# Scatter-add into the residual's table, and the last norm's roots on GpSimd, in a one-core decoder step with 32 experts

## What is computed

```
h2 = rms_norm(x, norm2_g) * (1 + sc2) + sh2
...
return (jax.nn.silu(xb @ w1[e]) * (xb @ w3[e])) @ w2[e]
...
contrib = y_rows[dest] * w_sorted[:, None]
return jnp.zeros((t, d), y_rows.dtype).at[tok_sorted].add(contrib)
...
x = x + g2 * y.reshape(n, t, d)
...
y_prompt = rms_norm(xp, final_norm_g)
y_sample = rms_norm(xs, final_norm_g)
```

## Time and profile before

| | |
|---|---|
| median of 3 runs | 1634.91 us (1634.49 to 1636.73) |
| the profiled execution | 1632.61 us |
| its span, first to last instruction | 1630.9 us |
| PE busy in the span | 1577.2 us (97%) |
| DVE, ACT, POOL busy | 1264.6, 804.3, 300.4 us |
| bytes moved | 368.71 MB, mean 226 GB/s |
| granted PE clock, mean | 0.993 |

### The profile page before, as it was taken

One profiled execution on the slowest core, in us unless ns is written; L12 is line 12 of the kernel. 1 busy time (PEld: TensorE's weight loads), 2 busy tenths in 40 slices (PEclk: granted clock), 3 DMA queues, 4 the chain that ended last, 5 costly groups with the idle time before them and its releaser, 6 DMA issues.

```text
span 1630.9 us, 23361 instructions
## 1 busy us (share of the span) xinstructions
PE 1577.2 (97%) x9163; PEld 1347.6 (83%) x9163; DVE 1264.6 (78%) x1683; ACT 804.3 (49%) x867; POOL 300.4 (18%) x267
## 2 busy tenths in 40 slices
PE   6999999999999999999999999999999999999993
PEld 3777788788889999999899977888888888888871
DVE  4668887755838898877455469999999999999956
ACT  4222232334333223223243357778878888878832
POOL 2310000000000000002000205655432232233210
PEclk9999999999999999999999999999999999999997
DMA  9965222424434222224223648999999999999938
GB/s 339 317 205 169 86 82 87 149 78 148 127 97 162 92 84 79 79 85 144 59 78 97 232 176 320 379 405 400 392 388 383 383 377 384 378 381 394 363 149 319
DMA packets 217073, 368.71 MB, mean 226 GB/s; under 512 B 16338, under 2 KB 164898, under 8 KB 191610
## 3 DMA queue, kind: packets, MB, share of 16 engines
q1 hardware_dynamic: 198972, 332.41, 56.9%
q0 software_dynamic: 17344, 32.64, 5.6%
q10 hardware_dynamic: 646, 2.15, 0.3%
HBM read 353.63 MB, written 31.31 MB: 236 GB/s over the span
## 4 chain that ended last, share of the span: by engine, by line
PE 89%; DVE 6%; DMA 2%; DVEq 1%; issue 1%; ACT 1%; SPq 0%; POOLq 0%
PE z L2712 16%; PE z L2714 16%; PE z L2713 16%; PE z L825 7%; PE z L823 7%; PE z L824 7%; PE z L840 4%; PE z L842 4%; PE z L841 4%; PE q L814 2%; PE q L2603 2%; PE q L2622 1%; DVE conv L2134 1%; DMA ada_h<-in_w_ada_dram 1%; PE q L831 1%
## 5 line engine op out<-in xcount | busy, mean ns | idle before, releaser
L1146 DVE TENSOR_TENSOR wl<-wr,whr 128x2048 fp32r<-128x2048 f32 x198 | 446.5, 2283 | 0.0
L2712 PE MATMUL z<-h_hi,w_hi 128*128 128x272 f32 (+1 forms) x1248 | 407.2, 326 | 2.3 <-DVE h_lo L1953 1.8
L2714 PE MATMUL z<-h_hi,w_lo 128*128 128x272 f32 (+1 forms) x1248 | 402.9, 323 | 0.0
L2713 PE MATMUL z<-h_lo,w_hi 128*128 128x272 f32 (+1 forms) x1248 | 401.9, 322 | 0.0
L992 ACT ACTIVATE whr<-wr 128x2048 fp32r<-128x2048 f32 x198 | 374.9, 1911 | 51.9 <-PE z L825 51.3
L1953 DVE TENSOR_TENSOR w_lo<-w_raw,w_hi 128x1024 fp32r<-128x1024 f32 (+1 forms) x168 | 179.5, 1069 | 138.3 <-ACT w_hi L1652 138.3
L2712 PEld LDWEIGHTS z<-h_hi,w_hi 128*128 128x128 f32 x1248 | 234.9, 188 | 28.2 <-issue 7.3
L2714 PEld LDWEIGHTS z<-h_hi,w_lo 128*128 128x128 f32 x1248 | 234.7, 188 | 16.5
L2713 PEld LDWEIGHTS z<-h_lo,w_hi 128*128 128x128 f32 x1248 | 235.1, 188 | 15.7 <-issue 0.2
L823 PE MATMUL z<-whr,xTh 128*128 128x512 f32 x528 | 209.1, 396 | 0.1
L825 PE MATMUL z<-wl,xTh 128*128 128x512 f32 x528 | 206.4, 391 | 0.0
(11 more groups left out here) (452 smaller groups left out, 2278.7 us busy)
## 6 DMA issues: line engine op xcount, KB each, us to landing
wr<-in_w_dram SPq DMA_DIRECT2D x198, 1024.0 KB, 8.8
w_raw<-in_w_in_dram SPq DMA_DIRECT2D x104, 512.0 KB, 3.7
ada<-in_w_ada_dram SPq DMA_DIRECT2D x6, 2048.0 KB, 14.9
w_raw<-in_w_branch_dram SPq DMA_DIRECT2D x48, 256.0 KB, 2.7
w_raw<-in_w_out_dram SPq DMA_DIRECT2D x16, 512.0 KB, 3.9
yin<-y_rows SPq DMA_DIRECT2D x16, 512.0 KB, 9.8
ada_h<-in_w_ada_dram SPq DMA_DIRECT2D x2, 2048.0 KB, 14.8
ada_u<-in_w_ada_dram SPq DMA_DIRECT2D x2, 2048.0 KB, 9.8
```

The costliest lines, as they stand in the source:

```text
L1146: return dve.tensor_tensor(out, a, b, op)
L2712: pe.matmul(out, w_hi[w][:, k, :], hi[:, k, t0:t1], start=(k == 0), stop=False)
L2713: pe.matmul(out, w_hi[w][:, k, :], lo[:, k, t0:t1], start=False, stop=False)
L2714: last = pe.matmul(out, w_lo[w][:, k, :], hi[:, k, t0:t1], start=False, stop=(k == kn - 1))
```

## The change

Four edits are made together.

1. A block's results are added to the residual's own table `x1_dram` by the transfer itself (`compute_op=ALU.add`), at the row's index in the token list instead of the two-place list. As two experts can name one row, each scatter first waits until the one before has landed. `y_dram` is gone. The sample rows of the table are first zeroed by a POOL transfer, and the samples' residual goes to a small table `x1s_dram`, since their gate is applied at the end. At the end SP loads one tile of finished sums for each row tile, 9 transfers for 18, and the load of `x1a` falls away, and so do PE's sums and DVE's `row_sum`, except for the samples' product and sum.
2. The inverse roots are made by POOL in three batches of three tiles, 15 instructions each, with the tiles in the order 0, 1, 8, 2 to 7. ACT squares every tile straight from `yin`.
3. `factor_columns` and `factors_read` stand one pair of products later.
4. `bias_rows` stands before `gated(NB_B, GB0, 4)` instead of behind it.

```diff
             def scatter_dma(s, col, done):
-                pool.indirect_dma_start(y_dram, bass.IndirectOffsetOnAxis(ap=col, axis=0), ysb[s][:], None,
-                                        bounds_check=2 * TPAD - 1, oob_is_err=False).then_inc(done, 16)
+                pool.indirect_dma_start(x1_dram, bass.IndirectOffsetOnAxis(ap=col, axis=0), ysb[s][:], None,
+                                        bounds_check=TOK - 1, oob_is_err=False, compute_op=ALU.add).then_inc(done, 16)
...
             def scatter(b):
                 pool.wait_ge(m_y, b + 1)
-                scatter_dma(b % 2, tb0[:, b:b + 1] if b < NE else xcol[:, 0:1], m_sc[b % 2])
+                if b:
+                    pool.wait_ge(m_sc[(b - 1) % 2], 16 * ((b + 1) // 2))
+                scatter_dma(b % 2, tok0[:, b:b + 1] if b < NE else xtok[:, 0:1], m_sc[b % 2])
...
             for t in F_ORDER:
-                for k in range(2):
-                    r0 = t * P + k * TPAD
-                    sp.dma_start(yin[0:f_rows[t], t, k, :], y_dram[r0:r0 + f_rows[t], :]).then_inc(rows_in[t], 16)
+                sp.dma_start(yin[0:f_rows[t], t, :], x1_dram[t * P:t * P + f_rows[t], :]).then_inc(rows_in[t], 16)
...
-            sp.wait_ge(m_c, 8 + RN * (NCH // RN - 1) + 1)
-            sp.dma_start(x1a[:], x1_dram[0:SEQ, :].rearrange("(t p) d -> p t d", p=P)).then_inc(f_par, 16)
...
+            pool.dma_start(x1_dram[SEQ:TOK, :].rearrange("r (a c) -> r a c", c=64),
+                           blk64[0:SMP, 64:P].unsqueeze(1).to_broadcast([SMP, D // 64, 64])).then_inc(x1_out, 16)
...
+            def roots(n0, n):
+                v, y, t = fv[:, n0:n], fy[:, n0:n], ft[:, n0:n]
+                pool.wait_ge(f_sq, n)
+                pool.tensor_scalar(v, fss[:, n0:n], 1.0 / D, EPS, ALU.mult, ALU.add)
+                pool.drain()
+                pool.tensor_scalar(y.bitcast(I32), v.bitcast(I32), -0.5, float(MAGIC), ALU.mult, ALU.add)
+                pool.drain()
+                pool.tensor_scalar(v, v, -0.5, None, ALU.mult)
+                for _ in range(3):
+                    pool.drain()
+                    pool.tensor_tensor(t, y, y, ALU.mult)
...
+                last.then_inc(f_r, 1)
...
                     elif g and i == 2 * PT - 2:
                         spatial(PT, SMP)
+                    elif g:
                         factor_columns()
...
-                gated(NB_B, GB0, 4)
                 if g:
                     bias_rows()
+                gated(NB_B, GB0, 4)
                 inverse()
```

More of the change, by code:

```diff
@@ L112, in sb @@
             return t
-        F_PE, F_ORDER = (1, 3, 5, 7), (8, 1, 0, 3, 2, 5, 4, 7, 6)
-        F_BATCH = (F_ORDER[0:4], F_ORDER[4:9])
+        F_ORDER = (8, 0, 1, 2, 3, 4, 5, 6, 7)
+        F_BATCH = ((0, 1, 8), (2, 3, 4), (5, 6, 7))
+        F_ROWS = sum(F_BATCH, ())
         TG = [HALF, HALF + SMP]
@@ L309, in build @@
         top[0] = o
-        yin, o = at("yin", [P, NT, 2, D], F32, low_end)
+        yin, o = at("yin", [P, NT, D], F32, low_end)
         assert o <= whi_at
@@ L582, in build @@
         o_i, o_w, o_c, o_x, o_sc = (sem(n) for n in ("o_i", "o_w", "o_c", "o_x", "o_sc"))
-        f_par, g2_in, f_mm, m_w, f_sum, f_sq, f_y, f_out = (
-            sem(n) for n in ("f_par", "g2_in", "f_mm", "m_w", "f_sum", "f_sq", "f_y", "f_out"))
+        f_par, g2_in, m_w, f_sum, f_sq, f_r, f_y, f_out = (
+            sem(n) for n in ("f_par", "g2_in", "m_w", "f_sum", "f_sq", "f_r", "f_y", "f_out"))
         W_IN = ((v_out, 16), (mc_in, 32))
@@ L661, in moe_sync @@
                 r0 = (PT + t) * P
-                sp.dma_start(x1_dram[r0:r0 + rows, :], xres[0:rows, t, :]).then_inc(last_out[t % 2], 16)
+                dst = x1_dram[r0:r0 + rows, :] if t < PT else x1s_dram
+                sp.dma_start(dst, xres[0:rows, t, :]).then_inc(last_out[t % 2], 16)
             sp.wait_ge(r_ok, 1)
@@ L805, in moe_gpsimd @@
                     pool.wait_ge(m_y, n_)
-                    scatter_dma(0, xcol[:, 0:1], o_sc)
+                    pool.wait_ge(m_sc[0], 16 * ((NB + 1) // 2))
+                    pool.wait_ge(m_sc[1], 16 * (NB // 2))
+                    scatter_dma(0, xtok[:, 0:1], o_sc)
+            def roots(n0, n):
[9 more added lines that the diff above has]
+                    pool.tensor_tensor(t, y, y, ALU.mult)
+                    pool.drain()
+                    pool.tensor_tensor(t, v, t, ALU.mult)
+                    pool.drain()
+                    pool.tensor_scalar(t, t, 1.5, None, ALU.add)
+                    pool.drain()
+                    last = pool.tensor_tensor(y, t, y, ALU.mult)
+                last.then_inc(f_r, 1)
+            n = 0
+            for batch in F_BATCH:
+                roots(n, n + len(batch))
+                n += len(batch)
             pool.wait_ge(st_out, 16 * (3 + 2 * NS))
@@ L956, in moe_tensor @@
                         step_down(pe, c, whr[4 + c], wl[XS[4 + c]])
[L957 to L970, removed]
         def moe_scalar(act):
@@ L1060, in moe_scalar @@
                     factors(0)
[L1062 to L1076, removed]
+            for n, t in enumerate(F_ROWS):
+                rows = f_rows[t]
+                if t == NT - 1:
+                    act.wait_ge(f_sum, 1)
+                else:
+                    results_in(act, t)
+                if n >= 2:
+                    act.wait_ge(f_sq, n - 1)
+                act.activation(xg[n % 2][0:rows, :], yin[0:rows, t, :], ACT.Square,
+                               accum_out=fss[0:rows, n:n + 1]).then_inc(f_sq, 1)
         def pick_groups(dve, t0, t1):
@@ L1332, in moe_vector, with row_out @@
                     result(0)
[L1334 to L1339, removed]
-                results_in(dve, t)
[L1341 to L1372, removed]
+            dve.wait_ge(f_par, 16 * (2 + NS))
+            results_in(dve, NT - 1)
+            acc = yin[0:SMP, NT - 1, :]
+            tt(acc, acc, g2s[:], ALU.mult)
+            dve.drain()
+            tt(acc, acc, x1s[0:SMP, :], ALU.add).then_inc(f_sum, 1)
+            def row_out(t):
+                rows, out, n = f_rows[t], yin[0:f_rows[t], t, :], F_ROWS.index(t)
+                results_in(dve, t)
+                dve.scalar_tensor_tensor(out, out, fy[0:rows, n:n + 1], fgb[0:rows, :], ALU.mult, ALU.mult).then_inc(f_y, 1)
+            for n, batch in enumerate(F_BATCH):
+                dve.wait_ge(f_r, n + 1)
+                for t in batch:
+                    row_out(t)
         w_in_v = w_in[0].rearrange("(k p) c -> p k c", p=P)
@@ L1819, in _ @@
                 if g:
-                    act.wait_ge(x1_out, 16 * PT)
+                    act.wait_ge(x1_out, 16 * (PT + 1))
                 for i in range(CW):
@@ L2354, in _ @@
                 if g:
[L2355 removed]
+                    dve.wait_ge(x1_out, 16 * (PT + 1))
                 for i in range(CW):
@@ L2430, in _ @@
                         spatial(PT, SMP)
+                    elif g and i == 2 * PT - 1:
                         factors_read()
```

14 lines of the change are left out of this document (6 added, 8 removed).

## The result

The changed kernel takes **1644.71 us** (median of 5 runs, 1643.4 to 1646.24), the kernel before 1636.19 beside it on the same chip: a ratio of 1.0052 (95% interval 1.004 to 1.0064). It is 8.5 us slower, where 1620 was forecast. The profiled execution took 1646.14 us, its span is 1644.3: 13.4 more than before.

What follows compares the result with a forecast made beforehand. PE was taken as the bound, queues close behind, with one chain after the last scatter. The terms -2.2 - 3.1 + 1.0 - 11.0 = -15.3 gave 1619.6 us against the median 1634.9, rounded to 1620; range 1612 to 1637.

Steps and rivals of the forecast that it cites:

- Edits 3 and 4: Dense part: two waits of PE for late DVE reads go away, -2.2 and -3.1 us.
- The scatters beside PE: Expert part: the queues' reserve absorbs the adding scatters, cost 0; 0 to 5 us if partitions decide the engine.
- the map: Expert part: partitions 0 to 63 belong to engines 0 to 7, so 1.26 us a block instead of 0.63.
- price "as a gather": Expert part: adding reads destination rows as a gather does, +0.63 us of each engine a block.
- The reserve of "9 to 15 us": Expert part: backlog the chunk loads can bear before PE waits, 9 to 15 us, of which 1.5 used.
- the expert part becomes bound by its transfers: Rival, expert part: transfers make PE wait, whole gain lost at 1.73 us more a block, 1657 at 2.5; chance 0.13.
- Its formula: Expert part: at x us more per block, waiting is 29x - 3.6 - 19.3 less the reserve, 12.
- The new wait on POOL's queue: Expert part: each scatter waits for the one before, which lands with 8 us to spare; cost 0.
- The last scatter: Start of the end chain: reading before writing adds a DRAM trip, +1.0 us, between 0 and 3.98.
- The end: Behind the last scatter's landing: 32.2 us against 43.2, -11.0, with POOL's batches taking 4.7, 5.5 and 5.5 us.
- GpSimd's roots: Rival, at the end: POOL's instructions are 0.5 us apart, the end 6.9 us longer, 1626.5; chance 0.14.

Runs made afterwards that it cites:

- e1: The kernel before with only the two mended PE waits in the dense part (edits 3 and 4): 1628.13 us, ratio 0.9959.
- e2: The kernel after with scatters that write and do not add: 1630.4 us, ratio 0.9972.
- e6: The kernel before with a block's rows dealt over 16 groups of four partitions, as a control: 1634.92 us, ratio 0.9997.
- e4: The kernel after with a memset and one GpSimd integer instruction on scratch columns right behind the last scatter's issue: 1637.08 us, ratio 1.001.
- e10: e4 with float views in place of integer views in the new GpSimd instruction: 1636.72 us, ratio 1.0006.
- e11: The kernel after with e4's two instructions placed ahead of the loop over blocks, none behind the last scatter: 1643.95 us, ratio 1.0053.
- e7: e4 with DVE starting its multiplications only when all three batches of roots are made: 1640.5 us, ratio 1.0024.
- e3: The kernel after with a block's rows dealt over 16 groups of four partitions: 1630.52 us, ratio 0.9973.

## Why the prediction was wrong

Against the profiled execution it said 1617.3; 1646.14 came: 28.8 us too low. Step by step:

- *Edits 3 and 4* (-5.3): right. All blocks up to the ninth are 5.2 us early, and alone the mends gave 7.1 in the medians, 4.4 to 8.8 by its interval (e1; 4.6 in its trace, at every block).
- *The scatters beside PE* (0, with 0 to 5 us for the rows in the low partitions): this is the first step that failed, by 14.5 us. I had the mechanism only as a possibility, and undersized each of its terms.

  The addition costs 1.38 us a block and not 0.63 (e2). Two things that the trace of before held are missing in the 0.63. It was read from 1300 to 1500 us, where a block moves 57 rows; from 1018 to 1130 us it moves about 80, and queue 0 has 10.0% (the same in e6), so the same working gives 0.100 x 17.75 / 2 = 0.89. And it is the mean of 16 engines: if the low partitions belong to eight of them, as the map has it, these carry 64 of 80 rows, 1.6 times as much, which as an estimate is 1.42, close to the 1.38. The price "as a gather" was sound, for adding raised queue 0's share by 0.94 and 0.59 us a block in the two stretches, against 0.89 and 0.63 by that price; the stretch and the mean were not.

  The reserve of "9 to 15 us" is its low end: the landing stops at 24 to 26, 8 to 9.5 above the 16.5 at the start. In the later blocks I let the queues catch up by 0.92 us a block, as the earlier trace rows showed it; in e2 it is (12.6 - 7.7) / 6 = 0.82 (7.7 is the median of the chunks issued from 1231 us). With 1.38 that leaves 0.56 a block, and with the smaller later blocks less, but the blocks are 18.44 - 17.75 = 0.69 behind the plan. Why was not tried, and stays open.

  Of the rivals, "the expert part becomes bound by its transfers", at 0.13, has the mechanism. Its formula had the same faulty terms: at x = 1.38 it gives 29 x 1.38 - 3.6 - 19.3 - 12 = 5.1 us, and 14.5 were lost. By itself that loss would have ended near 1619.6 + 14.5 = 1634, at the time of before; slower than before it became only with the end.
- *The new wait on POOL's queue* (0): right, e2 has it and loses nothing.
- *The last scatter* (+1.0 between 0 and 3.98): +2.1 in the trace; against a plain one at the same place (3.2, e2) adding costs 2.9.
- *The end* (-11.0, that is 32.2 us behind the last landing): the second step that failed, by 13.0 us; it took 45.2. The loads and squares came as said, the first batch began 9.5 us behind the landing (9.4 forecast). But the first batch took 12.7 us for 4.7: its instructions were 0.35 us apart, near the 0.31 taken, and the gap of 7.7 was not counted (e4, e10 and e11 place it). The earlier trace rows took the spacing from two places without a gap, though the same POOL showed 6.74 and 5.02 us between them and 8.31 at 965 us. The other two took 8.0 for 5.5: I had a factor for POOL beside DVE, 1.2, from long work at another place, and missed that each of POOL's instructions waits for a whole multiplication (e7). Sum: 38.3 instead of 25.1.

The two failed steps, 14.5 and 13.0, and the scatter's 1.1 make the 28.8 within 0.2 us. GpSimd's roots were a rival with 0.14 and a price of 6.9; the slowness was not of every instruction, as that rival had it.

## What to carry to other kernels

When PE is the bound but the transfer engines are full beside it, any work added to them has a reserve in the landing times of the loads: measure how fast it is used up and where the ring of buffers ends it, and take the busiest engine, not the mean of sixteen. Read the price in the stretch where the load is highest. Where the rows of an indirect transfer lie matters: dealing them over all partitions was one line and took 13.2 us off the kernel after (e3), and nothing off the kernel before, where the queues had room (e6). A few small instructions at the end of a kernel are better left to DVE: GpSimd is free there, but here it started late behind indirect transfers, and stood still beside DVE's wide instructions.

## What was not expected of the hardware

- Adding in an indirect scatter cost the queues 0.70 us a block of about 80 rows when spread (0.94 by the share of queue 0), and 1.38 in the low partitions; the last one, with few rows, lands after 6.1 us, a plain one after 3.2.
- The second of GpSimd's ordinary instructions behind indirect transfers comes 7.6 to 9.6 us late (7.69 in the kernel after, 9.57 in e2, 8.97 in e4, 9.18 in e10, 7.57 in e11), whether on float or integer views, and again after an earlier gap of 5.46 (e11). GpSimd's first indirect transfer behind ordinary instructions came 8.31 us late in the kernel before.
- GpSimd's instructions of three columns are 0.35 us apart beside an idle DVE, and the first three take 1.04 to 1.29 us beside multiplications of 1.22.
- An adding scatter also costs POOL more to issue: 2.9 us for 2.2 in the blocks, 1.56 for 1.00 at the end.
